# Spreading four constant vectors and a gate with TensorE instead of broadcast DMAs, in a two-model kernel on one core

## The reference, cut to what matters

```python
m = (sc @ w_mod[i] + b_mod[i]).reshape(bsz, 6, d)     # sh1, s1, g1, sh2, s2, g2, each of width 1024
h_lat = x * (1.0 + s1) + sh1
def chunk_mlp(h, n_chunks, w_in, norm_g, norm_b, w_s, b_s, w_out):
    z = jax.nn.gelu(h @ w_in)
    u, v = jnp.split(z, 2, axis=-1)
    v = layer_norm(v, norm_g, norm_b)
    ...
    s = jnp.einsum('hpq,bnqhc->bnphc', w_s, vb) + b_s.T[None, None, :, :, None]
    return (u * s.reshape(bsz, t, A_WIDTH)) @ w_out
x = layer_norm(DN_ALPHA * x + g1 * mix_lat, ln_g[i, 0], ln_b[i, 0])
ffn_lat = peer_ffn(x * (1.0 + s2) + sh2, ...)         # gathers 128 rows of 8 KB per token
```

## Time and profile before

| | before |
|---|---|
| median of 3 runs | 3656.82 us (3655.15 to 3657.91) |
| profiled execution, its time | 3656.92 us |
| its span in the profile | 3655.0 us |
| PE busy | 3253.0 us (89%) |
| DVE busy | 2544.8 us (70%) |
| ACT busy | 1780.5 us (49%) |
| bytes moved by DMA | 1157.75 MB, mean 317 GB/s |
| first gather of the peer's rows | at 216.65 us |

### The profile page before, as it was taken

How to read it: one execution, slowest core, us unless ns; L and a number is a source line. 1 busy time by engine, 2 the same in 40 slices (tenths; PEclk the granted TensorE clock), 3 DMA queues, 4 the chain that set the end, 5 groups by cost and what they waited for, 6 DMA issues and landing times. The chain is left out here.

```text
span 3655.0 us, 38099 instructions
## 1 busy us (share of the span) xinstructions
PE 3253.0 (89%) x12784; PEld 2025.5 (55%) x12784; DVE 2544.8 (70%) x5132; ACT 1780.5 (49%) x3850; POOL 871.7 (24%) x778
## 2 busy tenths in 40 slices
PE   6878898898898889888888777889999999999998
PEld 3444444443354434446322222279877989988897
DVE  2577778877877787657776777578665658766665
ACT  2334544544554565544444444355464545555453
POOL 0024344444443445420444444400000000000000
PEclk8989999999999999999999999999999999999999
DMA  9979999999999999982999999966655656565554
GB/s 398 371 284 417 418 418 400 415 416 402 418 407 417 419 419 417 418 309 92 369 421 421 421 420 421 422 215 179 189 173 179 181 179 188 169 187 195 159 185 138
DMA packets 279210, 1157.75 MB, mean 317 GB/s; under 512 B 31027, under 2 KB 33587, under 8 KB 174566
## 3 DMA queue, kind: packets, MB, share of 16 engines
q0 software_dynamic: 110592, 805.36, 53.3%
q1 hardware_dynamic: 168038, 349.73, 29.1%
q10 hardware_dynamic: 384, 0.23, 0.0%
HBM read 1154.07 MB, written 1.15 MB: 316 GB/s over the span
## 5 line engine op out<-in xcount | busy, mean ns | idle before, releaser
L86 PE MATMUL psum<-rows,diag 128*128 128x512 f32 x3072 | 1483.6, 619 | 291.0 <-ACT diag L2201 289.7
L2157 DVE CUSTOM_DVE_ANT_0 rows<-rows,h 128x1024 f32<-128x1024 f32 x768 | 939.1, 1224 | 488.0 <-DMA rows<-in_p_uv,place 483.9
L2053 POOL DMA_INDIRECT rows<-in_p_uv,place x768 | 867.7, 1130 | 1401.6 <-PE psum L86 1090.1
L86 PEld LDWEIGHTS psum<-rows,diag 128*128 128x128 f32 x3072 | 558.0, 193 | 1129.6 <-ACT diag L2201 630.7
L2956 DVE TENSOR_TENSOR weights_low<-landing,weights_high 128x1024 fp32r<-128x1024 f32 x400 | 486.5, 1222 | 327.1 <-ACT weights_high L2903 324.3
L2903 ACT CAST weights_high<-landing 128x1024 fp32r<-128x1024 f32 x398 | 414.6, 1049 | 501.5 <-PE psum L86 344.1
L2188 ACT ACTIVATE acted<-dots 128x1 f32<-128x1 f32 x768 | 155.1, 202 | 877.4 <-DVE dots L2157 875.7
L86 PE MATMUL psum<-weights_high,hT_high 128*128 128x512 f32 x832 | 352.5, 424 | 15.3 <-DVE h L694 6.7
L2201 ACT ACTIVATE diag<-ident,weight 128x128 f32<-128x128 f32 x768 | 308.4, 402 | 70.7 <-PE psum L86 0.4
L86 PE MATMUL psum<-weights_high,hT_low 128*128 128x512 f32 x832 | 326.1, 392 | 0.0
L86 PE MATMUL psum<-weights_low,hT_high 128*128 128x512 f32 x832 | 326.0, 392 | 0.0
(11 more groups left out here) (460 smaller groups left out, 3933.2 us busy)
## 6 DMA issues: line engine op xcount, KB each, us to landing
landing<-in_w_in SPq DMA_DIRECT2D x192, 512.0 KB, 4.0
landing<-in_w_ff SPq DMA_DIRECT2D x128, 512.0 KB, 4.4
landing<-in_w_mod SPq DMA_DIRECT2D x48, 1024.0 KB, 9.1
landing<-in_a_w_in SPq DMA_DIRECT2D x64, 256.0 KB
landing<-in_w_br SPq DMA_DIRECT2D x32, 512.0 KB, 4.3
rows<-in_p_uv,place POOLq DMA_INDIRECT x768
lat_landing<-in_b_w_in SPq DMA_DIRECT2D x48, 256.0 KB
landing<-in_a_w_out SPq DMA_DIRECT2D x32, 256.0 KB
```

Of the source, the lines that this page charges most:

```text
L86: return k.nc.tensor.matmul(out, lhsT, rhs, start=first, stop=last)
L2053: k.nc.gpsimd.indirect_dma_start(rows[:, n % ROW_RING, :], None, k.given["p_uv"], bass.IndirectOffsetOnAxis(place[:, g % 4, c:c + 1], 0))\
L2157: V.tensor_tensor_reduce(u, u, token, 1.0, 0.0, ALU.mult, ALU.add, dots[:, g % 4, c:c + 1]).then_inc(dots_done, 1)
```

## The change

The four constant vectors are loaded as one row of 4 KB each, to partition 0 or 32 of the buffer's second row, right behind the load of x. PE spreads them in eight halves of 512 columns by matmuls with a row of ones, into banks 6 and 7 alternately, and ACT copies each half into place. Each matmul from the third on waits for the copy two before it, so that its bank is free. Two more halves spread the gate from `conditioned.m`, at slot 64. The first turns wait for the first eight copies, the first spatial product for all ten. The five broadcast DMAs of s = 0 are gone; those of s = 1 stay.

```diff
+    LINES = ((v_rows, 0, given["a_norm_g"]), (v_rows, 32, given["a_norm_b"]), (n_rows, 0, given["ln_g"][0, 0:1, :]),
+             (n_rows, 32, given["ln_b"][0, 0:1, :]))
+    EARLY, HALVES = 2 * len(LINES), 2 * len(LINES) + 2
+    def line_of(n):
+        if n < EARLY:
+            to, at, _ = LINES[n // 2]
+            return to[at:at + 1, 1, n % 2 * NC:(n % 2 + 1) * NC], k.ones[at:at + 1, :]
+        at = 32 * (n % 2)
+        return conditioned.m[at:at + 1, 1, :], k.ones[at:at + 1, :]
+    def half_of(n):
+        span = slice(n % 2 * NC, (n % 2 + 1) * NC)
+        return LINES[n // 2][0][:, n // 2 % 2, span] if n < EARLY else g_row[:, span]
+    def pe_lines(pe):
+        for n in range(HALVES):
+            yield 1 if n < EARLY else 64
+            if n == 0:
+                pe.wait_ge(lines_landed, 16 * len(LINES))
+            elif n == EARLY:
+                pe.wait_ge(conditioned.taken, 2)
+            if n >= 2:
+                pe.wait_ge(lines_set, n - 1)
+            line, ones = line_of(n)
+            matmul(k, k.psum[:, 6 + n % 2, :], ones, line, True, True).then_inc(lines_spread, 1)
+    def act_lines(act):
+        for n in range(HALVES):
+            yield 1 if n < EARLY else 64
+            act.wait_ge(lines_spread, n + 1)
+            S.copy(half_of(n), k.psum[:, 6 + n % 2, :]).then_inc(lines_set, 1)
...
     def sp_rows(sp, s):
-        if s == 1:
+        if s == 0:
+            yield AHEAD + 1
+            for to, at, src in LINES:
+                sp.dma_start(to[at:at + 1, 1, :], src).then_inc(lines_landed, 16)
...
-            for j, name in enumerate(("ln_g", "ln_b")):
-                sp.dma_start(n_rows[:, j, :], given[name][0, 0].partition_broadcast(P)).then_inc(n_rows_landed, 16)
...
@@ pe_turns
             for half in range(2):
+                if t == 0 and s == 0:
+                    pe.wait_ge(lines_set, EARLY)
@@ pe_spatial
             if n == 0 and s == 0:
                 pe.wait_ge(ws_landed, 32)
+                pe.wait_ge(lines_set, HALVES)
@@ scalar
-                                         score_copies(act, S.copy, s, 1), act_high(act, s))]
+                                         score_copies(act, S.copy, s, 1), act_high(act, s),
+                                         *(() if s else (act_lines(act),)))]
```

More of the change, by code:

```diff
@@ L273, in first_mix @@
     rows_spread = sem("h_rows_spread")
-    h_rows_landed, v_rows_landed, ws_landed, n_rows_landed, g_row_landed, m_rows_landed, keys_landed, keys_clear = [
-        sem(n) for n in ("h_rows_landed", "v_rows_landed", "ws_landed", "n_rows_landed", "g_row_landed", "m_rows_landed",
+    h_rows_landed, v_rows_landed, ws_landed, g_row_landed, m_rows_landed, keys_landed, keys_clear = [
+        sem(n) for n in ("h_rows_landed", "v_rows_landed", "ws_landed", "g_row_landed", "m_rows_landed",
                          "keys_landed", "keys_clear")]
@@ L281, in first_mix @@
         sem(n) for n in ("mix_spread", "mix_root", "v_set", "spatial_done", "mix_y_set", "h2_set")]
+    lines_landed, lines_spread, lines_set = [sem(n) for n in ("mix_lines_landed", "mix_lines_spread", "mix_lines_set")]
     scored, copied, x_normed = sem("scored"), [sem("scores_copied0"), sem("scores_copied1")], sem("x_normed")
@@ L323, in sp_rows @@
     def sp_rows(sp, s):
-        if s == 1:
+        if s == 0:
+            yield AHEAD + 1
+            for to, at, src in LINES:
+                sp.dma_start(to[at:at + 1, 1, :], src).then_inc(lines_landed, 16)
+        else:
             yield load_slot(s, 0)
@@ L329, in sp_rows @@
                 sp.dma_start(h_rows[:, j, :], row(s, part)).then_inc(h_rows_landed, 16)
-        yield load_slot(s, 4) + 0.5
-        if s == 1:
+            yield load_slot(s, 4) + 0.5
             sp.wait_ge(h2_set, 2)
-        for j, name in enumerate(("a_norm_g", "a_norm_b")):
-            sp.dma_start(v_rows[:, j, :], given[name][0].partition_broadcast(P)).then_inc(v_rows_landed, 16)
+            for j, name in enumerate(("a_norm_g", "a_norm_b")):
+                sp.dma_start(v_rows[:, j, :], given[name][0].partition_broadcast(P)).then_inc(v_rows_landed, 16)
         if s == 0:
@@ L347, in sp_rows @@
                   .then_inc(keys_landed, 16)
-        yield load_slot(s, 10) + 0.5 if s == 1 else 65
         if s == 1:
+            yield load_slot(s, 10) + 0.5
             sp.wait_ge(taken, 4)
-        else:
+            sp.dma_start(g_row[:, :], row(s, 2)).then_inc(g_row_landed, 16)
+        yield load_slot(s, 32) + 0.5 if s == 1 else 65
+        if s == 0:
             conditioned.wait_stored(sp, 3)
-        sp.dma_start(g_row[:, :], row(s, 2)).then_inc(g_row_landed, 16)
-        yield load_slot(s, 32) + 0.5
         sp.wait_ge(v_set, 2 * s + 2)
@@ L499, in tensor @@
     def tensor(pe, s):
-        return [Aside(work(pe, s)) for work in (pe_passes, pe_spatial, pe_turns, pe_scores)]
+        works = [work(pe, s) for work in (pe_passes, pe_spatial, pe_turns, pe_scores)]
+        return [Aside(work) for work in (works if s else [pe_lines(pe)] + works)]
     def group_end(s, g):
@@ L639, in dve_v_norm @@
         step.mark(V.reciprocal(inverse[:, 0:2], root[:, 0:2]))
-        dve.wait_ge(v_rows_landed, 32 * (s + 1))
+        if s == 0:
+            dve.wait_ge(lines_set, 4)
+        else:
+            dve.wait_ge(v_rows_landed, 32)
         for t in range(2):
@@ L669, in dve_rows @@
         dve.wait_ge(m_rows_landed, 32 * (s + 1))
-        dve.wait_ge(n_rows_landed, 32)
+        dve.wait_ge(lines_set, EARLY)
         dve.wait_ge(spatial_done, 4 * s + 4)
@@ L690, in dve_out @@
                 if n % 4 == 0:
-                    dve.wait_ge(g_row_landed, 16 * (s + 1))
+                    if s == 0:
+                        dve.wait_ge(lines_set, HALVES)
+                    else:
+                        dve.wait_ge(g_row_landed, 16)
                 step.settle()
```

## The result

| | before | changed |
|---|---|---|
| median, measured on one chip | 3656.3 us (3653.26 to 3659.33) | 3660.86 us (3658.6 to 3666.04) |
| ratio to before, 95% interval | | 1.0014 [1.0007, 1.002] |
| profiled execution, its time | 3656.92 us | 3659.54 us |
| first gather | 216.65 us | 222.54 us |
| bytes moved by DMA | 1157.75 MB | 1155.14 MB |

The changed kernel is slower by 4.6 us. That is within the 0.2% named before as what can be told from no change, but the interval of these runs excludes 1. The removed bytes are gone: 1157.75 − 1155.14 = 2.61 MB.

A forecast was written before the change was run, and what follows sets the result against it. A full DMA queue bounds the kernel through the first gather. At chunk 34, 6.3 - 5.2 = 1.1 us; plus 1.0 for the clock, minus 0.5 for new waits, gives 1.6 us faster: 3655 us, range 3650 to 3661.

The forecast's parts named there:

- The lines hold PE longer: Rival, chance 0.25: clock stays at half in the lines' phase, queue empty for 8 us; 3658 to 3662 us.
- the forecast's own path: Whole kernel: 0 to 4 us faster, 3653 to 3657 us, chance 0.40.
- The rival's point of decision: DMA queue during the lines' phase: the kernel is slower once the queue is empty for more than 6.3 us.
- SP's two issues wait for it: Behind the copies, SP's a_w_in 6 issue slips to about 52.0 us and the next, `w_mod`, to about 52.9 us.
- the first spatial product waits for the gate's copies: Copies end at 117.1 to 117.5 us, PE arrives at 117.6: costs nothing, up to 1 us if chunk 31 is late.
- The step that failed: Lines' phase on PE: busy from 43.1 us, its clock rises within the phase, so halves and copies end at 51.0 us.
- my own half-clock bound: Lines' phase at half clock throughout: copies end at 52.6 us, PE 6.5 us late; 8 us of queue lost.
- The chain behind it: First turns to first weights pass on PE: 4.7 us, so the pass starts at 55.7 us and PE is 3.7 us late.
- The hole: DMA queue empty from 47.9 us until 52 to 53.4 us: 5.2 us lost, between 4 and 8 us.
- The small loads: Four 4 KB loads behind x, costed at nothing; as a rival at the page's price, chance 0.04, 3658 us.
- The bytes: Five broadcasts, 2.62 MB, removed from a full DMA queue ahead of chunk 34: 6.3 us earlier if the queue stayed full.
- The clock at that product: Second spatial product: a shorter wait may hold PE's clock, worth 1.8 us or 0; taken as 1.0 us.

The follow-up runs named there:

- bytes only: Against the changed kernel: POOL fills the four constant vectors with 0.5, without loading or spreading them; PE still spreads the gate. Median 3652.13 us, ratio 0.9985 to before.

## Why the prediction was wrong

The direction was wrong, and the rival *The lines hold PE longer* was right in its mechanism: the clock stays at half, PE is late, the queue runs empty. Its price, 3658 to 3662 us, holds the measured 3660.86 too, but in part by luck: its own sum had the stream 1.7 us late, and the second spatial product came 5.2 us late. The measured time also lies just inside the stated range of 3650 to 3661 us, which owes it to this rival; the forecast's own path went the other way. The rival's point of decision, slower from a hole of 6.3 us on, can't be told by the times: with a hole of 6.7 us the ratio is 1.0004, with 2.2 us 0.9994, and neither interval excludes 1.

**What held.** The bound of the end of this stretch is the DMA queue, read through the second spatial product and the first gather; the phase begins when the cast of chunk 1 ends (predicted 42.5 us, seen 43.5); SP's two issues wait for it; the first spatial product waits for the gate's copies (0.63 us in the changed kernel), and the wait of 4.17 us ahead of the second one hides this, as the prediction had it; the gate brings about what its bytes are worth. Where lines and gate are both spread by PE, the second spatial product follows the hole: 127.27 us (bytes only, whose 0.2 us is within the reading's error) plus a hole of 0.4, 2.2, 6.7, 7.3, 9.9 and 10.0 us gives 127.7, 129.5, 134.0, 134.6, 137.2 and 137.3 us, and 126.89, 129.82, 132.87, 134.14, 136.63 and 136.41 were seen.

**The step that failed** is "PE is now busy from 43.1 us on, so it should rise within the phase. I take 51.0 us." The clock stayed at 0.50 through the phase and beyond it, to about 60 us. I had read the rise near 53 us in the earlier trace rows as a matter of PE being busy, whatever it did. In the run over 128 rows the clock rose inside the phase and in those over 1 and 32 it did not, which settles that the rows in use matter; by what mechanism, the runs don't show. The Trainium skill, "TensorE: Matmul & The Clock Gate", section "What's actually happening", says that the clock is throttled by default and that activity releases it. The traces agree for the products with a `w_mod` chunk, which came to the full clock by 18.14 us in the kernel before, but not for every activity: with halves over one row between the same products, 34 us of unbroken work stayed at the half clock. What followed from the step:
- The phase: halves and copies end at 52.6 us by my own half-clock bound, at 54.0 in fact. The start was 1.0 us later (chunk 1 landed at 42.9 us and not at 41.9, 0.6 us of it by the small loads), and the phase itself 0.4 us longer. Turns at 54.12, not 51.0.
- The chain behind it: 7.05 us (54.12 to 61.17), where I had 4.7; the 4.75 us of the run over 128 rows shows that the 4.7 was right for the full clock. The third `w_mod` chunk on PE stands at 64.12 us against 54.96 in the earlier trace rows: PE is 9.2 us late, not 3.7, and beyond the 6.5 of my half-clock bound too, by the 1.5 us that the turns are behind 52.6 and a chain still longer than I had put it.
- The hole: 9.9 us, not 5.2 (bound 8).

**Terms off in size.** The small loads: nothing predicted, 0.6 us measured for four. The prediction's estimate of 2.7 us from the Trainium skill, "DMA: Bandwidth & Descriptors", section "Bandwidth", which would have given 3658 us, was too much by a factor of four. The bytes: 6.3 us predicted, 4.1 us at the second spatial product by the bytes-only run. The clock at that product: I took +1.0 us for a shorter wait, but with a wait of 4.17 us the product took 3.75 us again, as with 6.03: 0. With waits of 3.83 to 3.99 us it took 2.82 to 3.40 us in four of the other kernels, which fits the idea; the wait was not short enough for it. The sum with measured terms: −4.1 (bytes, and no lines) + 9.9 (hole) + 0.6 (loads) = 6.4 us later at the second spatial product; 5.2 were seen, and the 1.2 us between them stay unexplained.

The clock alone does not turn the sign. With the forecast's own hole of 5.2 us the measured bytes and loads give −4.1 + 5.2 + 0.6 = 1.7 us later, no gain either, and the run over 128 rows, whose clock rose inside the phase, still had its second spatial product 2.7 us later than before. So two steps failed: the clock, which made the hole 9.9 us, and the removed bytes, put at 6.3 us of which 4.1 arrived.

**Left open.** Where the missing 2.2 us of the removed bytes go in the bytes-only kernel: between 61 and 125 us its queue moves 394 GB/s where before moved 398, some 0.6 us of it, and between 30 and 61 us 400 GB/s where before moved 412, another 0.9 us; the rest, and why the queue is slower, isn't traced. And why the first eight gathers moved by 5.9 us while the ninth moved by 3.6 and the next ones by 3.0. It is not that a wait takes up the lateness: in the bytes-only kernel, which was 4.3 us early, the ninth is 6.8 us early. The wait ahead of the ninth gather is 16.2 us in the profiled execution of the kernel before and 13.9 us in the changed one, and what sets it wasn't tested.

## What to carry to other kernels

Before giving work to an idle stretch of TensorE, look at when the engines that it hands over to are free, and at what SP has queued behind them: here the stretch was idle on PE, but ACT stood in a cast for the first half of it, and two `w_mod` issues were waiting behind. Price matmuls with one or few rows at the half clock, put lines on four partition groups so that they run side by side, and place them where PE waits for its very first input; the kernel that did the last two together, and used six banks, gained 4.4 us. To price a hole in a full DMA queue, add up the missing shares of its windows: here each microsecond came back nearly whole 70 us later.

## What the runs showed of the hardware

- Matmuls over 1 or 32 rows left TensorE's clock at 0.50 (1.2 GHz) for the whole of a phase of 10 us, and for 34 us when they alternated with products of two columns; the same matmuls over 128 rows brought it to 0.90 in the window at 49 to 51 us, and the full clock by 51 us. The products of two columns by themselves reached the full clock (1.04 us at 18.14 us in the kernel before).
- Two halves (matmuls of 1x512 in f32) of one partition group took 3.78 us at half clock, about 1.8 us each; four on four groups took about 2.1 us together from 9.04 us on. This agrees with the Trainium skill, "TensorEngine Tiling (Array Packing)", section "Key Properties", which has tiles work independently. That stretch was read as PEclk 1.00, but its neighbour product took 1.89 us, the half clock's time: ahead of the first recorded change the row isn't to be trusted.
- Four loads of 4 KB, each to a single partition, in a full queue cost 0.6 us together.
